# Two wide matmul pieces behind every second step of a scan's recurrence, in place of one behind each

## What is computed

```python
def rwkv7_scan(r, decay, k, v, kk, a, s0, reverse):
    xs = tuple(jnp.moveaxis(t.astype(jnp.float32), 1, 0) for t in (r, decay, k, v, -kk, kk * a))

    def step(s, inp):
        r_t, w_t, k_t, v_t, a_t, b_t = inp
        sa = jnp.einsum('bhvk,bhk->bhv', s, a_t)
        s = s * w_t[:, :, None, :] + sa[..., None] * b_t[:, :, None, :] + v_t[..., None] * k_t[:, :, None, :]
        return s, jnp.einsum('bhvk,bhk->bhv', s, r_t)

    s_last, ys = lax.scan(step, s0, xs, reverse=reverse)
    return jnp.moveaxis(ys, 0, 1), s_last
...
for z in range(2):
    yc_z, s_ctx = rwkv7_scan(rc, dc, kdc, vc, kkc, ac, s0, z == 1)
    yx_z, _ = rwkv7_scan(rx, dx, kdx, vx, kkx, ax, s_ctx, z == 1)
```

## Time and profile before

| | |
|---|---|
| median of 3 runs | 2486.53 us (2483.26 to 2489.89) |
| profiled execution, its own time | 2488.11 us |
| its span, first to last instruction | 2486.3 us |
| mean granted TensorE clock | 0.992 |
| TensorE busy | 2415.5 us |
| VectorE, ScalarE, GpSimd busy | 1338.3, 790.2, 748.4 us |

### The profile page before, as it was taken

One profiled execution on the slowest core, in us unless ns is written; L12 is line 12 of the kernel. 1 busy time (PEld: TensorE's weight loads), 2 busy tenths in 40 slices (PEclk: granted clock), 3 DMA queues, 4 the chain that ended last, 5 costly groups with the idle time before them and its releaser, 6 DMA issues.

```text
span 2486.3 us, 65623 instructions
## 1 busy us (share of the span) xinstructions
PE 2415.5 (97%) x28580; PEld 1775.9 (71%) x28580; DVE 1338.3 (54%) x2764; ACT 790.2 (32%) x1612; POOL 748.4 (30%) x730
## 2 busy tenths in 40 slices
PE   6999999999999998899999999999999999999998
PEld 1566666666666666658888888865558888875797
DVE  4766666666666665454563333834624434545553
ACT  3354544445454443221221121013510014022312
POOL 2533433343434442100001034400055400540381
PEclk9999999999999999899999999999999999999999
DMA  7111111111111113544336732220134444332343
GB/s 302 49 39 45 42 39 48 41 46 39 39 39 39 50 37 124 188 169 153 136 133 213 269 120 89 91 84 30 43 130 171 146 145 139 136 120 72 98 153 110
DMA packets 80148, 258.30 MB, mean 104 GB/s; under 512 B 11639, under 2 KB 16984, under 8 KB 79096
## 3 DMA queue, kind: packets, MB, share of 16 engines
q1 hardware_dynamic: 75304, 242.94, 28.5%
q0 software_dynamic: 1360, 5.89, 0.7%
q10 hardware_dynamic: 3200, 5.27, 0.6%
HBM read 253.02 MB, written 1.05 MB: 102 GB/s over the span
## 4 chain that ended last, share of the span: by engine, by line
PE 55%; DVE 2%; DMA 1%; ACT 0%; issue 0%; SPq 0%; DVEq 0%; ACTq 0%
PE ps L2327 9%; PE ps L2125 9%; PE ps L2050 9%; PE ps L1975 7%; PE ps L2180 4%; PE ps L2105 3%; PE ps L2376 2%; PE ps L2225 2%; PE ps L2393 1%; PE ps L1895 1%; PE ps L2245 1%; PE ps L2210 1%; PE ps L2265 1%; PE ps L2204 1%; DMA ring<-in_w_mods 1%; PE ps L2083 1%
## 5 line engine op out<-in xcount | busy, mean ns | idle before, releaser
L2050 PE MATMUL ps<-h,ring 128*128 128x256 f32 x1024 | 225.6, 379 | 0.0
L2050 PEld LDWEIGHTS ps<-h,ring 128*128 128x128 f32 x1024 | 193.9, 190 | 34.9 <-issue 9.9
L1053 ACT ACTIVATE general<-general 64x512 f32<-64x512 f32 x160 | 101.8, 636 | 164.8 <-DVE general L1252 162.2
L583 PE MATMUL ps<-general,ring 128*128 128x512 f32 x256 | 134.9, 623 | 0.8 <-issue 0.8
L3515 POOL TENSOR_TENSOR general<-h 128x1024 f32<-128x1024 f32 (+1 forms) x4 | 7.2, 1803 | 423.8 <-DVE general L3255 238.0
L599 PE MATMUL ps<-general,ring 128*128 128x512 f32 x256 | 134.1, 629 | 0.0
L774 PEld LDWEIGHTS ps<-general 64*64 64x64 f32 (+1 forms) x5120 | 77.5, 130 | 68.8 <-issue 44.9
L2180 PE MATMUL ps<-ring,h 128*128 128x512 f32 x256 | 110.2, 592 | 0.0
L2327 PE MATMUL ps<-general,ring 128*128 128x256 f32 (+1 forms) x576 | 106.3, 327 | 0.6 <-DVE general L3328 0.6
L3509 POOL TENSOR_TENSOR general<-general 128x256 f32<-128x256 f32 x16 | 12.7, 796 | 310.2 <-ACT general L2550 310.2
L1252 DVE STREAM_TRANSPOSE general<-general 128x512 f32<-128x512 f32 x160 | 104.3, 690 | 2.2
(11 more groups left out here) (440 smaller groups left out, 5329.7 us busy)
## 6 DMA issues: line engine op xcount, KB each, us to landing
ring<-in_w_mods SPq DMA_DIRECT2D x88, 512.0 KB, 4.4
ring<-in_w_feature SPq DMA_DIRECT2D x74, 512.0 KB, 3.2
ring<-in_w_rkvg SPq DMA_DIRECT2D x64, 512.0 KB, 3.7
ring<-in_w_in SPq DMA_DIRECT2D x48, 512.0 KB, 3.2
ring<-in_w_merge SPq DMA_DIRECT2D x48, 512.0 KB, 4.2
ring<-in_w_out SPq DMA_DIRECT2D x32, 512.0 KB, 6.5
ring<-in_w_token SPq DMA_DIRECT2D x24, 512.0 KB, 4.8
ring<-in_w_merge SPq DMA_DIRECT2D x48, 256.0 KB, 2.7
```

Source lines behind the costliest of these rows:

```text
L583: mm = pe.matmul(ps[:, 0, :], W.wt[:, 0, k, :], W.mix_k[:, k, :], start=(k == 0), stop=(k == KD - 1))
L1053: last = act.activation(W.U[g:g + 64, 1], W.X0[a:a + 64, 1], ACT.Copy)
L2050: mm = pe.matmul(ps[:, n % 4, 0:NX], weights(key, k), R.h[:, k, 0:NX], start=(k == 0), stop=(k == KD - 1))
```

## The change

`FILL_STATES` becomes 512, and `fill` is called behind the even steps alone.

```diff
-FILL_STATES = 256
+FILL_STATES = 512
...
         for n in range(1, NCH - 1):
             for z in range(2):
                 advance(i, z, n)
-            fill(part, FILL_STATES)
+            if n % 2 == 0:
+                fill(part, FILL_STATES)
```

## The result

| | before | changed |
|---|---|---|
| median of the runs beside each other | 2485.03 us (4 runs) | 2499.61 us (4 runs, 2497.99 to 2499.91) |
| ratio | | 1.0054, 95% interval 1.0037 to 1.0072 |
| profiled execution, own time and span | 2488.11, 2486.3 us | 2497.99, 2496.2 us |
| recurrence of iteration 2, first advance to L887 | 5.72 us | 6.73 us |

The change makes the kernel slower: by 0.54% by the ratio, and by 14.6 us between the two medians. The two profiled executions lie only 9.9 us apart, since the one of before is among the longest of its kernel and the one of the change the shortest of its four; the medians are what is compared here.

What follows compares the result with a forecast made beforehand. TensorE's queue was taken as the bound: three bare steps 2.61, two long 2.78 and the last 1.48 make 6.87 us against 5.72, +17.3 us over 15 iterations on 2486.5. Forecast 2503.8 us, range 2494 to 2511.

Steps and rivals of the forecast that it cites:

- The bound: Whole kernel: TensorE has 2415.5 us of work, 97% of the span; whatever lengthens its queue lengthens the kernel unless waits shrink.
- The sign that went with it: Changed profile: TensorE's busy time stays near 2415 us and its idle time grows by 17.
- A filled step with a second piece: Even recurrence steps, two pieces behind each: 1.39 us, the last 1.48 up to the reads, the round trip hidden.
- A bare step: Steps 1, 3 and 5 without a piece: 0.87 us each, as in iteration 15, nearly what a step with its piece takes.
- the low bound: Bare step of 0.80 us, recurrence 6.66 us, +0.94 an iteration, +14.1 in all: 2500.6 us.
- The sum: Recurrence of iterations 0 to 14: 6.87 us against 5.72, +1.15 in each of 15, +17.3 us in all.
- a sign of being wrong: Changed profile: the forecast is wrong if the bare step is under 0.8 us.
- Why the bare pair is late: Iteration 15's bare pair: its weight load starts only 0.03 us ahead of the matmul, against 0.11 covered; the load waits too.
- VectorE's queue: Recurrence: packing done before scalings 3 and 5; GpSimd's 0.40 us delay falls on covered scaling 4, the 0.20 stall goes.
- A, absorbed behind it: Rival: waits of L774 and L1907 behind the recurrence shrink, giving 2496.4 us, or 2488.6 with both; chance 0.09.
- B, not bare: Rival: the round trip fits within the pair's issue, recurrence 5.49 us, 2483.1 or 2475.7 us; gains below 0.49; chance 0.04.
- C, the clock: Rival: idle in bare steps lowers TensorE's clock, 3.5 us a fall, 2556 us if every iteration, 2521 every third; chance 0.05.

Runs made afterwards that it cites:

- four_bare: Kernel before, with three pieces behind steps 3 and 6 and steps 1, 2, 4 and 5 bare: 2510.68 us, ratio 1.0100.
- packing_swapped: Kernel before, with VectorE's packing operations behind scalings 3 and 4 exchanged: 2485.35 us, ratio 0.9996; run again, 2483.49 us, ratio 0.9984.
- one_bare: Kernel before, with only step 1 bare, two pieces behind step 2 and one behind each of the rest: 2489.59 us, ratio 1.0017.
- all_behind: Kernel before, with all six pieces behind the last step, so five steps are bare: 2543.25 us, ratio 1.0233.
- directions_swapped: Changed kernel, with direction 1 (ScalarE's) first in each advance pair: 2500.89 us, ratio 1.0062 against the kernel before.
- all_behind_swapped: packing_swapped, with all six pieces behind the last step: 2540.09 us, ratio 1.0211 against the kernel before.

## Why the prediction was right

The measured median is 2499.61 us, 4.2 us under the forecast of 2503.8 and inside its range of 2494 to 2511. Of these 4.2, 1.5 are the median of the kernel before, which came out at 2485.03 in place of 2486.53, and 2.1 are the bare step; the rest is within what medians scatter.

- **The bound.** TensorE's queue was the bound, and idle time added to it arrived: the fifteen recurrences of the two profiles differ by 15.2 us in all, and the medians by 14.6 and 16.2 us in two comparisons. The sign that went with it was off in size: TensorE's idle time was to grow by 17 us and its work to stay, and by the pages of the two profiles the idle time grew by 7.2 and the work by 2.7. Some 0.30 us of a recurrence's growth is counted as busy, and the wait of L1907 was 5.4 us shorter in the profile of the change.
- **A filled step with a second piece.** Forecast 1.39, measured 1.41 or 1.42; the last 1.48 against 1.50. Pairs 3 and 5 wait for nothing, as said.
- **A bare step.** This is the term that was mis-sized: "I take 0.87", measured 0.80, which was the low bound. The argument for 0.87 was that the bare pair is 0.07 us slower and gives the 0.07 back. It is slower: VectorE starts 0.45 us after pair 2 (260.07 to 260.52) and 0.37 after pair 1, and the wide piece starts 0.50 after it. But that lateness falls on a step with two pieces behind it. VectorE's part of it is covered there, and of TensorE's 0.09 the two pieces take back more than half: they go through in 0.92 us (260.57 to 261.49) where 0.97 was counted. Only 0.02 or 0.03 is left in the long step. The 0.87 itself is right where a bare step follows a bare one: four_bare has 0.87 and 0.88 there. The sum had 6.87 us for what is 6.73, +17.3 us for +15.2. The prediction named a bare step under 0.8 us as a sign of being wrong; it came out on that edge, at 0.79 or 0.80.
- **Why the bare pair is late.** The prediction read this rightly. The load of the weights starts 0.03 ahead of the matmul (260.04 and 260.07), also in the change, and the trace's record of that load carries the wait for the state itself. The two passes of direction 0 then start 0.13 us apart (260.07 and 260.20), with the second pass's load between them, against 0.06 in pair 3 (261.49 and 261.54), which waits for nothing. That is the 0.07 or 0.08 us by which VectorE starts later. The fifth pair of the kernel before, delayed by the stall of step four, shows the same (load, matmul at 261.31, scaling):

```profile
261.27 0.52 PEld L877 LDWEIGHTS ps<-general 128*128 128x128 f32 x4 [0.40 <-issue]
...
261.75 0.28 DVE L1280 TENSOR_SCALAR general<-ps,general 128x64 f32<-128x64 f32 x1 [0.26 <-PE ps L877]
```

  With the stall taken away (packing_swapped, above) that pair's load starts 0.11 ahead (261.76 and 261.87) and VectorE 0.37 after the pair, not 0.44. So the sum came out near the low bound, but not by the way that the prediction took from the Trainium skill (TensorE: Matmul & The Clock Gate, step-by-step). That page tells of loads pulled ahead of matmuls in flight; here the load itself had to wait, so these rows are no test of it.
- **VectorE's queue.** Right: the fourth step's stall is gone. The prediction said that the 0.40 us of delay would fall on scaling 4 in a long step. It did not occur at all. GpSimd's product waits for ScalarE's copy after its state 2, and the long second step lets nearly all of it pass (261.43 to 262.16) before the packing operation behind scaling 3 starts (262.06). one_bare shows the same with the second step alone long.
- **A, absorbed behind it.** Did not happen. L774's wait is 7.9 us in both. The prediction priced it too high, as 7.9 / 16 = 0.49 us each: one of the 16 is 1.5 us long, in the last iteration, and the fifteen usual ones are 0.43, 6.4 us together in place of 7.4. L1907's wait was shorter in the two profiles of the change, and the medians show nothing given back by it; it varies nearly as much between two executions of one program.
- **B, not bare.** Did not happen: 0.80 us is far from the 0.49 at which the change would have begun to gain.
- **C, the clock.** It did not fall in any recurrence of iterations 0 to 14 with one or two bare steps together. With five it did: 25 us of all_behind's 58 (1.69 us more in iteration 2 than in iteration 0, 9.57 against 7.88, fourteen times, and 1.5 more in iteration 1, which took 11.05). The Trainium skill (TensorE: Matmul & The Clock Gate, A second HAM failure mode: psum-queue depth-cycling) tells of a clock that swings when the engine idles briefly and often between groups of matmuls. all_behind agrees with it, at 1.00, 0.69 and 0.82 in its first three recurrences; the change, at 1.00 in all fifteen, doesn't show it. No run separates the short waits from the small share of wide work as the cause.

## What to carry to other kernels

Filler work between the steps of a recurrence pays only as far as it covers the round trip of the step it stands behind: a piece of 0.49 us behind each step hid 0.39 us of waiting every time, and two pieces in one place hid the same 0.39 once. Before moving filler, look for a place in the same trace where the chain runs bare (here the last iteration) and read the step there, but take it behind the same kind of neighbour. If filler is short, leave bare the step whose successor doesn't need it at once (the last one here cost 0.13 us in place of 0.39), and don't put five bare ones in a row.

## What was not expected of the hardware

- A bare step behind covered work is 0.80 us, behind another bare one 0.87 (four_bare), with the same instructions. The pair behind a wait starts its passes 0.13 us apart in place of 0.06.
- VectorE's operations of 128x512 and of 128x256, each with two inputs from SBUF, are both slowed by 0.40 us beside GpSimd's product of 0.73 us: 0.68 to 1.08 and 0.42 to 0.82. The scaling of 128x64 out of PSUM is not: it took 0.29 us at 260.43, while the product started at 260.44. In directions_swapped VectorE's L1201 was there first (262.00 to 262.68): it kept its 0.68 us, and the product that started at 262.25 took 1.02 in place of 0.73.
- The clock held with two bare steps between wide work and fell with five, in fourteen of fifteen recurrences. In all_behind iteration 0 was spared, in all_behind_swapped, with 0.28 us less waiting, iteration 8. In iteration 2 of all_behind it was at 1.00 through the steps with their waits and at 0.61 in the dense work behind them.
